# First feed-forward matrix of a two-layer decoder by Strassen's seven block products

## The chip, the cores and the metric

One program on one NeuronCore of a Trainium2 chip. The metric is the device time of one execution in microseconds. In the profile PE is TensorE, DVE VectorE, ACT ScalarE, POOL GpSimd and SP SyncE, which here only issues transfers.

## What is computed

Two layers of a decoder trunk on 1024 prompt tokens and 8 sample tokens, 1032 columns in all. The part that the change touches is the feed-forward block of each layer:

```python
h = _rmsnorm(x, w['norm_ffn_g'][l])
gu = jnp.einsum('bld,df->blf', h, w['ffn_w_up'][l])
gate, up = gu[..., :D_FF], gu[..., D_FF:]
gate, ffn_buf = _causal_dwconv(gate, st_ffn_conv[l], w['ffn_conv_w'][l], w['ffn_conv_b'][l])
x = x + jnp.einsum('blf,fd->bld', jax.nn.gelu(gate) * up, w['ffn_w_down'][l])
```

D_MODEL is 1024 (8 tiles of 128), D_FF 2816 (22 tiles), the convolution has width 3. Ahead of it in a layer stands the mixer: an input projection of 32 tiles, three groups of heads (linear recurrence, retention, state space) and an output projection. It is the same before and after.

## The kernel before

Activations lie feature by token: `x[:, m, :]` is tile m of the residual stream, 128 features by 1032 tokens. Each operand of a large product is split in a high part (rounded to the matmul's fp32r type) and the rest, and each product takes three matmuls (`three`, L695 to L697): high by high, rest by high, high by rest. A token row is cut in NG = 3 groups of 344 columns, since a PSUM bank holds 512.

**Weights.** A slot is 128 x 1024 floats, eight 128 x 128 blocks: one output tile of the first matrix over all of D_MODEL, or a part of the second. SP loads it into one half of `w_raw`, GpSimd splits it into `w_hi` (L674) and `w_lo` (L677) in a loop over all slots of the program, and TensorE frees it. A layer has 44 slots for the mixer and 6 for each of FB = 11 feed-forward blocks.

**Feed-forward blocks.** A block makes two tiles of `gate` and the same two of `up` (four slots, each 8 x 9 matmuls into three PSUM banks), and then two slots of the second matrix for the block ahead of it, eight pieces that are added to `x`. VectorE takes a gate tile out of PSUM with the norm factor `rstd` (L1952), adds two conv taps to what ScalarE's first tap left (L1959, and L1962 for the 8 sample columns), takes the up tiles out (L1970), adds the pieces to `x` (L1992), multiplies gate and up (L1978), and makes the rest of the product's split (L1986). Nine blocks run in a hardware loop; the first and the last are written out.

**The turn.** The mixer's last slots (`out` 5 and two `fin` slots) add the output projection to `x`, tile by tile, in pieces of 344 columns (L1488). As soon as a tile is whole, ScalarE squares it (L1107) and makes the high part of the tile scaled with its norm gain (L1111); VectorE adds the square to `rstd` (L1443) and makes the rest (L1454). `h_hi` and `h_lo` hold all 8 tiles. The division by the token norm comes later, when a product leaves PSUM.

What sets the order is the program of each engine, written by hand, with semaphores between them.

## Time and profile before

| | |
|---|---|
| median of 3 runs | 2878.07 us (2877.52 to 2882.84) |
| span of the profiled execution, first to last instruction | 2875.8 us |
| its own time | not recorded apart; the runs are 1.7 to 7.0 us above the span |
| mean granted TensorE clock | 0.990 |
| TensorE busy | 2817.4 us (98%), 18198 matmuls |
| VectorE, ScalarE, GpSimd busy | 58%, 20%, 36% |
| DMA moved | 228 MB, mean 79 GB/s |

A row that groups instructions names line, engine, operation, output and inputs by the program's names, the shape and the count, then busy time and the mean of one in ns, then the engine's idle time just before them. A source row gives the shortest, middle and longest duration in ns. A timeline row has the start in us, how long it was busy, and what it waited for in brackets. A stretch row has for each engine the busy us and the count, then the granted clock. Matmuls are pipelined: each lasts some 320 ns while one starts every 157, so a pace is read from starts, not from durations.

### The profile page before, as it was taken

To read this page: it belongs to the slowest core of one execution; us is meant where nothing else is said; L and a number is where in the kernel's file an instruction comes from. 1 tells how busy PE (TensorE), PEld (TensorE's weight loads), DVE (VectorE), ACT (ScalarE), POOL (GpSimd) and SP (SyncE) were. 2 spreads that over 40 slices of the span, in tenths; PEclk is the share of its full clock that TensorE was granted. 3 is DMA by queue.
4 is the path that set the end of the run, shared out by engine and by line. 5 is a ranking of instruction groups with operands and counts; after the bars stand their busy time and mean duration, and the time that the engine had idled before them with its cause. 6 is when DMAs were issued, how large, how long until landed. Compare 5 with 4: busy or idle time off the path is not lost.

```text
span 2875.8 us, 46926 instructions
## 1 busy us (share of the span) xinstructions
PE 2817.4 (98%) x18198; PEld 2759.6 (96%) x18198; DVE 1661.4 (58%) x2108; ACT 589.3 (20%) x902; POOL 1022.4 (36%) x440
## 2 busy tenths in 40 slices
PE   9999999899999999999999999998999999999998
PEld 9999999889999999999999999998899999999997
DVE  7659886467344444444746597855664444444447
ACT  4334231123000111001313333211221100111002
POOL 2333323213434434434434333232243443443432
PEclk9999999999999999999999999999999999999998
DMA  4325324411111111111123334344011111111112
GB/s 159 129 79 154 130 92 162 156 33 44 45 51 44 44 51 44 49 46 44 56 89 106 126 113 146 115 135 141 31 46 52 44 46 49 44 47 48 44 52 87
DMA packets 76113, 228.08 MB, mean 79 GB/s; under 512 B 18704, under 2 KB 19728, under 8 KB 74912
## 3 DMA queue, kind: packets, MB, share of 16 engines
q1 hardware_dynamic: 71600, 210.79, 22.5%
q10 hardware_dynamic: 4368, 15.33, 1.7%
q8 instruction: 94, 1.54, 0.2%
q14 instruction: 51, 0.42, 0.0%
HBM read 180.63 MB, written 45.96 MB: 79 GB/s over the span
## 4 chain that ended last, share of the span: by engine, by line
PE 88%; DVE 5%; issue 4%; DMA 1%; ACT 1%; POOL 0%; DVEq 0%; SPq 0%; POOLq 0%; ACTq 0%
PE ps L695 27%; PE ps L697 26%; PE ps L696 26%; DVE sb_pt L1498 2%; PE ps L807 1%; DMA sb_raw<-proj 1%; PE ps L809 1%; PE ps L924 1%; PE ps L863 0%; PE ps L812 0%; PE ps L925 0%; PE ps L830 0%; PE ps L842 0%; PE ps L841 0%; PE ps L882 0%
## 5 line engine op out<-in xcount | busy, mean ns | idle before, releaser
L695 PE MATMUL ps<-sb_h_hi,sb_w_hi 128*128 128x344 f32 x3840 | 1239.6, 323 | 3.5 <-DVE sb_h_lo L1454 1.5
L696 PE MATMUL ps<-sb_h_lo,sb_w_hi 128*128 128x344 f32 x3840 | 1226.3, 319 | 0.0
L697 PE MATMUL ps<-sb_h_hi,sb_w_lo 128*128 128x344 f32 x3840 | 1225.9, 319 | 0.0
L674 POOL TENSOR_TENSOR sb_w_hi<-sb_w_raw,sb_ones 128x1024 fp32r<-128x1024 f32 x218 | 426.2, 1955 | 1795.3 <-PEq L1054 860.4
L695 PEld LDWEIGHTS ps<-sb_h_hi,sb_w_hi 128*128 128x128 f32 x3840 | 722.5, 188 | 12.9 <-issue 7.7
L696 PEld LDWEIGHTS ps<-sb_h_lo,sb_w_hi 128*128 128x128 f32 x3840 | 722.6, 188 | 1.0
L697 PEld LDWEIGHTS ps<-sb_h_hi,sb_w_lo 128*128 128x128 f32 x3840 | 722.5, 188 | 0.0
L677 POOL TENSOR_TENSOR sb_w_lo<-sb_w_raw,sb_w_hi 128x1024 fp32r<-128x1024 f32 x218 | 596.1, 2734 | 17.1
L695 PE MATMUL ps<-sb_y_hi,sb_w_hi 128*128 128x344 f32 x1440 | 476.2, 331 | 20.6 <-DVE sb_x L1488 14.5
L697 PE MATMUL ps<-sb_y_hi,sb_w_lo 128*128 128x344 f32 x1440 | 465.2, 323 | 0.0
L696 PE MATMUL ps<-sb_y_lo,sb_w_hi 128*128 128x344 f32 x1440 | 462.4, 321 | 0.0
L1992 DVE TENSOR_TENSOR sb_x<-ps,sb_x 128x1032 f32<-128x1032 f32 x168 | 207.0, 1232 | 242.3 <-PE ps L697 242.3
L695 PEld LDWEIGHTS ps<-sb_y_hi,sb_w_hi 128*128 128x128 f32 x1440 | 273.5, 190 | 27.0 <-DVE sb_x L1488 16.4
L696 PEld LDWEIGHTS ps<-sb_y_lo,sb_w_hi 128*128 128x128 f32 x1440 | 273.9, 190 | 1.1
L697 PEld LDWEIGHTS ps<-sb_y_hi,sb_w_lo 128*128 128x128 f32 x1440 | 273.7, 190 | 0.0
L1485 DVE TENSOR_TENSOR sb_ev<-ps,sb_rstd 128x344 f32<-128x344 f32 x180 | 89.5, 511 | 218.0 <-PE ps L697 214.3
L1952 DVE TENSOR_TENSOR sb_raw<-ps,sb_rstd 128x1032 f32<-128x1032 f32 x44 | 54.3, 1234 | 255.8 <-PE ps L697 255.5
L1410 ACT ACTIVATE sb_y_hi<-sb_pt 128x1032 fp32r<-128x1032 f32 x40 | 42.9, 1073 | 732.2 <-DVE sb_pt L1978 732.2
L1970 DVE TENSOR_TENSOR sb_pt<-ps,sb_rstd 128x1032 f32<-128x1032 f32 x44 | 54.2, 1233 | 234.6 <-PE ps L697 234.6
L1488 DVE TENSOR_TENSOR sb_x<-ps,sb_x 128x344 f32<-128x344 f32 x264 | 127.0, 511 | 52.5 <-PE ps L697 51.8
L1959 DVE SCALAR_TENSOR_TENSOR sb_pt<-sb_raw,sb_par,sb_pt 128x1024 f32<-128x1024 f32 x88 | 128.0, 1455 | 7.1 <-DVE sb_pt L1962 5.6
L1403 ACT ACTIVATE sb_pt<-sb_raw,sb_par 128x1032 f32<-128x1032 f32 x44 | 55.3, 1256 | 328.8 <-DVE sb_raw L1952 328.8
(256 smaller groups left out, 2249.5 us busy)
## 6 DMA issues: line engine op xcount, KB each, us to landing
sb_w_raw<-w SPq DMA_DIRECT2D x222, 512.0 KB, 3.6
proj<-sb_ev SPq DMA_DIRECT2D x64, 516.0 KB, 3.0
sb_pt<-proj SPq DMA_DIRECT2D x28, 516.0 KB, 5.0
sb_raw<-proj SPq DMA_DIRECT2D x16, 516.0 KB, 4.6
sb_raw<-proj ACTq DMA_DIRECT2D x16, 516.0 KB, 4.2
...
```

The costliest lines, as they stand in the source:

```text
L674: nc.gpsimd.tensor_tensor(w_hi[:, q, :], w_raw[:, q, :], ones[:, 0:1].to_broadcast([P, 1024]), ALU.mult).then_inc(sg.sem("w_hi_done"), 1)
L677: nc.gpsimd.tensor_tensor(w_lo[:, q, :], w_raw[:, q, :], w_hi[:, q, :].bitcast(F32), ALU.subtract).then_inc(sg.sem("w_split_done"), 1)
L695: mm(o, wh, ah, start=first, stop=False)
L696: mm(o, wh, al, start=False, stop=False)
L697: return mm(o, wl, ah, start=False, stop=last)
L1403: af(pt[:, j, :], raw[:, j, 2:T + 2], ACT.Identity, bias=wt[3], scale=wt[2]).then_inc(*sg.on("ffn_tap", (tag, j)))
L1485: v.tensor_tensor(ev[:, EV[i], gc(g)], o, rstd[:, gc(g)], ALU.mult).then_inc(*sg.on(f"p_free{r % NB}", r))
L1488: v.tensor_tensor(x[:, mo, gc(g)], o, x[:, mo, gc(g)], ALU.add).then_inc(*sg.on(f"p_free{r % NB}", r))
L1498: ins = stt(dst[:, 0:SEQ], src[:, k:k + SEQ], w(k), dst[:, 0:SEQ], ALU.mult, ALU.add)
L1952: v.tensor_tensor(g3(raw[:, j, 2:T + 2]), ffn_bank(r)[:, :, 0:TG], g3(rstd[:]), ALU.mult).then_inc(*sg.on("m_free", ("ffn", r)))
L1959: stt(pt[:, j, 0:SEQ], raw[:, j, k:k + SEQ], w, pt[:, j, 0:SEQ], ALU.mult, ALU.add).then_inc(*line.step())
L1992: v.tensor_tensor(g3(x[:, mo, :]), ffn_bank(r)[:, :, 0:TG], g3(x[:, mo, :]), ALU.add).then_inc(*sg.on("m_free", (tag, r)))
```

## The change

It computes the first feed-forward matrix by Strassen's scheme. The product of two output tiles is seen as 2 x 2 blocks: weights A11, A12, A21, A22 (two output tiles by two halves of D_MODEL, 128 x 512 each), activations in two halves of D_MODEL by two halves of the tokens (H = 516). Seven products of four 128 x 128 blocks by 516 columns, each in two groups of HG = 258, take the place of eight. They are called by the activation panel that they use, in the order I1, I5, I2, I6, I7, I3, I4.

- **TensorE.** `product` runs 4 x 2 x 3 matmuls of 258 columns into two banks. `up_pair` runs the seven of a pair, each behind a wait for the eviction that frees its banks; a block has two pairs, gate and up. The second matrix is computed as before, in pieces of 344 columns.
- **Panels.** Instead of `h_hi`/`h_lo`, seven panels `p_hi`/`p_lo` of 4 x 516 columns are made once per layer, at the turn: I1, I2 and I3 are quarters of scaled `x`, I5, I6, I7 and I4 use sums of quarters (t1 to t4). VectorE makes the sums and the rests, ScalarE the high parts. Squares for the norm go through three buffers and are added by GpSimd (tiles 1 to 3) and VectorE (4 to 7). Memory of the mixer is reused for the panels.
- **Weights.** The ring now has three places of 128 x 512, an entry each: 14 entries for a block's first matrix, 4 for its second (22 of either kind in the last block). GpSimd makes four sums for each pair and the rest of every entry; ScalarE makes the high parts (`hi`), each released by the end of the product three entries earlier. SP's loads (three places of 1024) are released by GpSimd's rests.
- **VectorE in a block.** A pair's seven products leave PSUM in seven half-row additions (`c11`, `add_p6`, `c22`, `c12`, `c21`, with a running sum in `tab`). They no longer multiply by `rstd`: the gate tiles are scaled by it in place (`scaled`), and GELU's output too (`scale_gelu`); the product of both is made in `raw` (`times_gelu`).
- **Next layer.** The constants are loaded again in each layer, and GpSimd splits the next layer's first two slots in halves between the last pieces.

```diff
+H = T // 2
+HG = H // 2
+I1, I2, I6, I5, I7, I4, I3 = range(7)
+PER_BLOCK, LAST_ENTRIES = 18, 22
 
...
 
-        pairs = DEPTH * SLOTS // 2 - 1
-        with pool.Fori(0, pairs) as i, sg.loop("split", pairs, i):
-            for q in range(2):
-                pool.wait_ge(sg.sem(f"w_raw{q}"), i * 16 + 32)
-
-                pool.wait_ge(sg.sem(f"w_used{q}"), i + (1 + q))
-                nc.gpsimd.tensor_tensor(w_hi[:, q, :], w_raw[:, q, :], ones[:, 0:1].to_broadcast([P, 1024]),
-                                        ALU.mult).then_inc(sg.sem("w_hi_done"), 1)
-                pool.wait_ge(sg.sem("w_hi_done"), i * 2 + (q + 1))
...
+            def lo(b, e, src):
+
+                r = e if b is None else e + 2
+                pool.wait_ge(*seen("f_hi", layer, b, e + 1))
+                lo_of(w_place(w_lo, r), src, w_place(w_hi, r)).then_inc(sg.sem("f_lo"), 1)
...
+            def up_pair(b, pair):
...
+                nc.gpsimd.tensor_tensor(wsum[:], a21, a22, ALU.add).then_inc(sg.sem("f_sum"), 1)
+                lo(b, e, a11)
+                sums_done(b, n + 1)
+                nc.gpsimd.tensor_tensor(a21, a21, a11, ALU.subtract).then_inc(sg.sem("f_sum"), 1)
+                lo(b, e + 1, wsum[:])
+                sums_done(b, n + 2)
+                los_done(b, e + 2)
+                nc.gpsimd.tensor_tensor(a11, wsum[:], a11, ALU.subtract).then_inc(sg.sem("f_sum"), 1)
+                lo(b, e + 2, a12)
+                sums_done(b, n + 3)
+                los_done(b, e + 3)
+                nc.gpsimd.tensor_tensor(a12, a12, a11, ALU.subtract).then_inc(sg.sem("f_sum"), 1)
+                lo(b, e + 3, a11)
+                lo(b, e + 4, a21)
+                sums_done(b, n + 4)
+                lo(b, e + 5, a12)
+                lo(b, e + 6, a22)
+
...
+            def product(b, bank0, e, panel):
+
+                r = e if b is None else e + 2
+                wh, wl = w_place(w_hi, r), w_place(w_lo, r)
+                entry_ready(b, e)
+                for kk in range(4):
+                    if b is None and e < 7:
+                        pe.wait_ge(*sg.after("pn_lo", (panel, kk)))
+                    w = slice(kk * P, (kk + 1) * P)
+                    for g in range(2):
+                        n = slice(HG * g, HG * g + HG)
+                        ins = three(ps[:, bank0 + g, 0:HG], wh[:, w], wl[:, w], p_hi[:, panel, kk, n],
+                                    p_lo[:, panel, kk, n], kk == 0, kk == 3)
+                        weights_done()
+                ins.then_inc(sg.sem("f_done"), 1)
...
+            def up_pair(b, pair):
+                e, n = 7 * pair, 7 * pair
+                if pair:
+                    pe.wait_ge(*seen("f_ev", layer, b, 5))
+                    if b is None:
+                        pe.wait_ge(*sg.after("rstd_ready", "ffn"))
+                elif b is not None:
...
+                pe.wait_ge(*seen("f_copy", layer, b, pair + 1))
+                product(b, P1_BANK[pair], e + 4, I7)
+                if b is None and pair == 0:
+                    pe.wait_ge(*sg.after("tok_rstd", "ffn"))
+                pe.wait_ge(*seen("f_ev", layer, b, n + 1))
+                product(b, P2_BANK, e + 5, I3)
+                if b is None and pair == 0:
+                    ffn_spread()
+                pe.wait_ge(*seen("f_ev", layer, b, n + 2))
...
+            def hi(b, e, ahead=0):
+
+                if b is not None or e > 2:
+                    act.wait_ge(*seen("f_done", layer, b, turn(e - 3) if e > 2 else e - 2, ahead))
+                elif e != 1:
+                    act.wait_ge(sg.sem(f"w_used{e // 2}"), layer * PAIRS + PAIRS)
...
+            act.wait_ge(*sg.after("sqf_pool", 3))
+            square_f(5, raw[:, 0, 2:T + 2])
+            x_done(7)
+            hi_x(I2, 3, 7, n0)
+            hi(None, 2)
+            rest_panels(3)
+            act.wait_ge(*sg.after("pn_lo", (I4, 1)))
+            square_f(6, fpt[:, 0, :])
+            act.wait_ge(*sg.after("sqf_dve", 5))
+            square_f(7, raw[:, 0, 2:T + 2])
...
+            def up_block(b, blk, tag):
+                if b is not None:
+                    act.wait_ge(*seen("f_done", layer, b, 0))
+                    ys(b, y_hi, -2)
+                copy_p1(b, 0)
+                hi(b, 3)
+                hi(b, 4)
+                hi(b, 5)
...
+                for g in range(NG):
+                    evict(("out", 5, mo, g))
+                diff(mo)
+                if mo >= 1:
...
+                evict(("fin", 5 + kk, 2))
+                rest_lo(kk)
+            square_add(4, tab[:])
+            square_add(5, raw[:, 0, 2:T + 2])
+            lo_x(I2, 3, 7, n0)
+            make_t2(3)
+            make_t3_t4(3)
...
+            def c11(b, pair):
+                piece_done(b, 7 * pair + 3)
+                dve.wait_ge(*seen("f_copy", layer, b, pair + 1))
+                v.tensor_tensor(g2(raw[:, 0, 2:H + 2]), pair_bank(P2_BANK), g2(ta), ALU.add).then_inc(sg.sem("f_ev"), 1)
...
+            def up_block(b, blk, tag):
+                if b is not None:
+                    dve.wait_ge(*seen("f_split", layer, b, 0))
+                c11(b, 0)
...
+                scaled(0, rstd[:]).then_inc(sg.sem("f_gate"), 1)
+                c21(b, 0)
+                scaled(1, rstd[:]).then_inc(sg.sem("f_gate"), 1)
+                conv_gate(blk, tag, 0)
+                conv_gate(blk, tag, 1)
+                c11(b, 1)
+                scale_gelu(tag, 0)
+                add_p6(b, 1)
```

Three places of the engines' orders. First GpSimd in a looped block, where `sb_w_raw`, `sb_w_hi` and `sb_w_lo` are a slot as loaded, its high part and its rest, and `sb_wsum` a sum of two weight blocks. Before:

```order
L674 TENSOR_TENSOR sb_w_hi<-sb_w_raw,sb_ones 128x1024 [waits w_used0]
L676 ISA
L677 TENSOR_TENSOR sb_w_lo<-sb_w_raw,sb_w_hi 128x1024 [waits w_hi_done]
L673 REGISTER_ALU [waits w_raw1]
L674 TENSOR_TENSOR sb_w_hi<-sb_w_raw,sb_ones 128x1024 [waits w_used1]
```

Now, the second pair of a block:

```order
L824 TENSOR_TENSOR sb_wsum<-sb_w_raw 128x512 [waits f_lo,f_raw1,f_raw0]
L807 REGISTER_ALU
L785 TENSOR_TENSOR sb_w_lo<-sb_w_raw,sb_w_hi 128x512 [waits f_hi]
L814 REGISTER_ALU
L827 TENSOR_TENSOR sb_w_raw<-sb_w_raw 128x512 [waits f_sum]
L807 REGISTER_ALU
L785 TENSOR_TENSOR sb_w_lo<-sb_wsum,sb_w_hi 128x512 [waits f_hi]
L814 REGISTER_ALU
L831 TENSOR_TENSOR sb_w_raw<-sb_wsum,sb_w_raw 128x512 [waits f_lo,f_sum]
```

Every instruction has half the width, sums stand between the rests, and each rest waits for ScalarE's high part.

Second VectorE in a looped block, from the last gate eviction to the first of the up tiles. Before:

```order
L1952 TENSOR_TENSOR sb_raw<-ps,sb_rstd 128x1032 [waits ffn_stored1,m_ready]
L1955 ISA
L1959 ISA [waits ffn_tap]
L1959 SCALAR_TENSOR_TENSOR sb_pt<-sb_raw,sb_par,sb_pt 128x1024
...
L1962 SCALAR_TENSOR_TENSOR sb_pt<-sb_par,sb_pt 128x8
L1969 REGISTER_ALU
L1970 TENSOR_TENSOR sb_pt<-ps,sb_rstd 128x1032 [waits m_ready]
```

Now:

```order
L2447 TENSOR_TENSOR sb_raw<-ps,sb_tab 128x516 [waits f_done]
L2411 REGISTER_ALU
L2451 TENSOR_TENSOR sb_raw<-sb_raw,sb_rstd 128x1032 [waits f_ev]
L2454 ISA
L2458 ISA [waits ffn_tap]
L2458 SCALAR_TENSOR_TENSOR sb_fpt<-sb_raw,sb_par,sb_fpt 128x1024
...
L2461 SCALAR_TENSOR_TENSOR sb_fpt<-sb_par,sb_fpt 128x8
L2414 REGISTER_ALU
L2418 REGISTER_ALU [waits f_done]
L2419 TENSOR_TENSOR sb_raw<-ps,sb_tab 128x516 [waits f_copy]
```

A two-operand scaling of `sb_raw` (L2451) is new between them, and what stands behind the eight conv instructions is now `c11` (L2419), which frees banks for the third product after it.

Third ScalarE at the end of the turn (`sb_p_hi` are the panels' high parts, `sb_fpt` and `sb_tab` hold sums, squares and running sums). Now:

```order
L1646 ACTIVATE sb_p_hi<-sb_x,sb_gf 128x516 [waits p_free1]
L1680 ACTIVATE sb_w_hi<-sb_w_raw 128x512 [waits w_used1]
L1651 ACTIVATE sb_p_hi<-sb_raw 128x516 [waits pn_t] x2
L1651 ACTIVATE sb_p_hi<-sb_fpt 128x516 [waits pn_t]
L1732 ISA
L1654 ACTIVATE sb_fpt<-sb_x 128x1032 [waits pn_lo]
L1654 ACTIVATE sb_raw<-sb_x 128x1032 [waits sqf_dve]
L1646 ACTIVATE sb_p_hi<-sb_x,sb_gf 128x516 x4
L1749 ISA
L1754 ACTIVATE sb_tab<-ps 128x516 [waits sqf_dve,f_done]
L1678 REGISTER_ALU [waits f_done]
L1680 ACTIVATE sb_w_hi<-sb_w_raw 128x512 [waits f_sum]
```

The two rows of L1680 are the high parts of entries 2 and 3, for products I2 and I6. The first stands behind the panel of tile 7, the second behind the rest of the panels, two squares and the copy of the first product out of PSUM. Before, the same place:

```order
L1107 ACTIVATE sb_ev<-sb_x 128x1032 [waits sq_used,p_free2]
L1118 REGISTER_ALU
L1111 ISA [waits p_free1]
L1111 ACTIVATE sb_h_hi<-sb_x,sb_gains 128x1032
L1107 ACTIVATE sb_ev<-sb_x 128x1032 [waits sq_used,p_free1]
L1111 ISA
L1111 ACTIVATE sb_h_hi<-sb_x,sb_gains 128x1032
L1125 ACTIVATE sb_rt<-sb_rt 128x9 [waits tok_ms]
```

There ScalarE made only the last tiles' squares and high parts; weights have come in between.

## Rows read from the trace of the kernel before

**Rows 1.** The page: busy time of the engines, and the chain's lines.
```profile
PE 2817.4 (98%) x18198; PEld 2759.6 (96%) x18198; DVE 1661.4 (58%) x2108; ACT 589.3 (20%) x902; POOL 1022.4 (36%) x440
...
PE ps L695 27%; PE ps L697 26%; PE ps L696 26%; DVE sb_pt L1498 2%; PE ps L807 1%; DMA sb_raw<-proj 1%; PE ps L809 1%; PE ps L924 1%; PE ps L863 0%; PE ps L812 0%; PE ps L925 0%; PE ps L830 0%; PE ps L842 0%; PE ps L841 0%; PE ps L882 0%
```

**Rows 2.** Busy time in a stretch of the first layer's feed-forward part.
```profile
core 0: us, PE busy (x) PEld busy (x) DVE busy (x) ACT busy (x) POOL busy (x), PEclk, DMA share, GB/s
760.00:1360.00 600.00, 600.00 (x3826) 600.00 (x3825) 270.91 (x211) 58.86 (x53) 242.41 (x106) 1.00 0.15 47
```

**Rows 3.** Timeline of TensorE, sixteen narrow matmuls and what follows.
```profile
310.98 1.95 PE L863 MATMUL ps<-sb_con,sb_pt 128*128 128x128 f32 x16
312.68 0.40 PE L695 MATMUL ps<-sb_h_hi,sb_w_hi 128*128 128x344 f32 x1
```

**Rows 4.** Source lines of GpSimd's rests and of two VectorE products.
```profile
L677 POOL TENSOR_TENSOR sb_w_lo<-sb_w_raw,sb_w_hi x218: 2347/2406/4263, 31.5 to 2831.8; 128x1024 fp32r<-128x1024 f32 x109
L1978 DVE TENSOR_TENSOR sb_pt<-sb_pt x44: 1850/2134/3444, 730.4 to 2810.6; 128x1032 f32<-128x1032 f32 x44
L1986 DVE TENSOR_TENSOR sb_y_lo<-sb_pt,sb_y_hi x40: 1221/1227/1236, 735.5 to 2768.9; 128x1032 fp32r<-128x1032 f32 x40
```

**Rows 5.** Timeline of GpSimd, one slot.
```profile
797.04 1.89 POOL L674 TENSOR_TENSOR sb_w_hi<-sb_w_raw,sb_ones 128x1024 fp32r<-128x1024 f32 x1 [6.95 <-PEq L1054]
799.01 3.29 POOL L677 TENSOR_TENSOR sb_w_lo<-sb_w_raw,sb_w_hi 128x1024 fp32r<-128x1024 f32 x1
```

**Rows 6.** Timeline of VectorE, the same place.
```profile
798.05 5.34 DVE L1978 TENSOR_TENSOR sb_pt<-sb_pt 128x1032 f32<-128x1032 f32 x2
803.31 1.22 DVE L1986 TENSOR_TENSOR sb_y_lo<-sb_pt,sb_y_hi 128x1032 fp32r<-128x1032 f32 x1
```

**Rows 7.** Source lines of VectorE: additions from PSUM, conv taps.
```profile
L1992 DVE TENSOR_TENSOR sb_x<-ps,sb_x x168: 1219/1233/1234, 777.1 to 2851.7; 128x1032 f32<-128x1032 f32 x168
L1488 DVE TENSOR_TENSOR sb_x<-ps,sb_x x264: 494/511/519, 131.9 to 2101.7; 128x344 f32<-128x344 f32 x132
L1959 DVE SCALAR_TENSOR_TENSOR sb_pt<-sb_raw,sb_par,sb_pt x88: 1279/1286/1964, 707.7 to 2792.6; 128x1024 f32<-128x1024 f32 x88
L1962 DVE SCALAR_TENSOR_TENSOR sb_pt<-sb_par,sb_pt x88: 225/227/2267, 709.7 to 2794.0; 128x8 f32<-128x8 f32 x88
```

**Rows 8.** Source lines of ScalarE: 1032 and 512 columns.
```profile
L1107 ACT ACTIVATE sb_ev<-sb_x x40: 1047/1068/1073, 17.3 to 2853.0; 128x1032 f32<-128x1032 f32 x40
L1202 ACT ACTIVATE sb_ch<-sb_ch x32: 630/631/636, 258.5 to 1835.7; 128x512 f32<-128x512 f32 x32
```

**Rows 9.** The page: DMA issues of the weight slots.
```profile
sb_w_raw<-w SPq DMA_DIRECT2D x222, 512.0 KB, 3.6
```

**Rows 10.** Busy time in the first layer's turn.
```profile
668.00:700.00 32.00, 32.00 (x215) 31.96 (x215) 20.27 (x20) 6.56 (x7) 14.62 (x6) 1.00 0.22 53
```

**Rows 11.** Timeline of VectorE in that turn.
```profile
668.78 2.69 DVE L1443 TENSOR_TENSOR sb_rstd<-sb_rstd,sb_ev 128x1032 f32<-128x1032 f32 x1
671.39 3.43 DVE L1454 SCALAR_TENSOR_TENSOR sb_h_lo<-sb_x,sb_gains,sb_h_hi 128x1032 fp32r<-128x1032 f32 x1
```

**Rows 12.** Timeline of TensorE behind an idle stretch in the mixer.
```profile
573.11 0.65 PE L695 MATMUL ps<-sb_y_hi,sb_w_hi 128*128 128x344 f32 x1 [4.99 <-DVE sb_x L1488]
573.56 0.49 PE L696 MATMUL ps<-sb_y_lo,sb_w_hi 128*128 128x344 f32 x1
573.85 0.49 PE L697 MATMUL ps<-sb_y_hi,sb_w_lo 128*128 128x344 f32 x1
```

**Rows 13.** Busy time and granted clock around it.
```profile
560.00:568.00 8.00, 8.00 (x57) 7.61 (x55) 5.56 (x5) 3.83 (x5) 5.16 (x2) 1.00 0.85 290
573.00:582.00 9.00, 8.08 (x27) 7.64 (x28) 6.72 (x11) 0.26 (x1) 0.00 (x0) 0.50 0.17 58
```

More of the change, by code:

```diff
@@ new lines, in _ @@
+            with sp.Fori(0, LOOPED) as b, sg.loop("ffn", LOOPED, b):
+                ffn_up_weights(b)
+                for j in range(2):
+                    gate_row(b, j, "loop")
+                taken(b, 12)
+                ffn_weights(b, 5)
+            ffn_up_weights(LOOPED)
+            for j in range(2):
+                gate_row(LOOPED, j, "end")
+            taken(LOOPED, 12)
+            ffn_weights(LOOPED, 5)
+            taken(LOOPED, 13)
+            ffn_weights(LOOPED, 6)
+            taken(LOOPED, 15)
@@ new lines, in mixer_left, with ffn_sums @@
+            def mixer_left(bank0):
+                for b_ in range(bank0, bank0 + 2):
+                    last = max(r for r in RING.values() if r % NB == b_)
+                    pe.wait_ge(*sg.after(f"p_free{b_}", last))
+            def ffn_sums():
+                pe.wait_ge(*sg.after("sqf_dve", KD - 1))
+                pe.wait_ge(*seen("f_ev", layer, None, 1))
+                for c in range(NCH + 1):
+                    s = slice(c * CHUNK, min((c + 1) * CHUNK, T))
+                    ins = mm(ps[0:s.stop - s.start, 2, c:c + 1], rstd[:, s], ones[:, 0:1], start=True, stop=True)
+                ins.then_inc(*sg.on("tok_sum", "ffn"))
@@ L1115, in refresh @@
             square(m, key)
[L1116 to L1120 removed]
+            if m == KD - 2:
+                act.wait_ge(sg.sem("f_done"), layer * PIECES + PIECES)
             part(m, g, key)
@@ L1418, in A_dyn, with copy_p1 @@
                 return out
-            ffn_block(0, "first", 0)
-            with act.Fori(0, LOOPED) as b, sg.loop("ffn", LOOPED, b):
-                ffn_block(b + 1, "loop", b * 12 + 4)
-            ffn_block(FB - 1, "end", END + 4)
-            for m in range(KD):
-                act.wait_ge(*freed(layer, END + 12 + m))
-                refresh(m, layer * 2 + 2, "next")
+            def copy_p1(b, pair):
+                act.wait_ge(*seen("f_done", layer, b, 7 * pair + 1))
+                if b is not None or pair:
+                    act.wait_ge(*seen("f_ev", layer, b, 7 * pair - 1))
+                else:
+                    act.wait_ge(*sg.after("sqf_dve", 4))
+                af(g2(ta), pair_bank(P1_BANK[pair]), ACT.Identity).then_inc(sg.sem("f_copy"), 1)
@@ new lines, in _ @@
+            up_block(None, 0, "first")
+            for e in range(3):
+                hi(0, e)
+            with act.Fori(0, LOOPED) as b, sg.loop("ffn", LOOPED, b):
+                up_block(b, b + 1, "loop")
+                for e in range(14, PER_BLOCK):
+                    hi(b, e)
+                for e in range(3):
+                    hi(b, e, 1)
+            up_block(LOOPED, FB - 1, "end")
+            for e in (14, 15, 16):
+                hi(LOOPED, e)
+            ys(LOOPED, p3_hi, 0)
@@ L1427, in _, with next_tile @@
+            hi(LOOPED, 17)
+            hi(LOOPED, 18)
+            def next_tile(m):
+                act.wait_ge(*d_freed(layer, LOOPED, 5 + m))
+                refresh(m, layer * 2 + 2, "next")
+            next_tile(0)
+            hi(LOOPED, 19)
+            next_tile(1)
+            next_tile(2)
+            hi(LOOPED, 20)
+            next_tile(3)
+            hi(LOOPED, 21)
+            for m in range(4, KD):
+                next_tile(m)
         root("last")
@@ L2005, in _, with evicted, piece_done @@
-            up_part(FB - 1, "end", END + 4, 0)
-            for j in range(2):
-                y_product("end", END + 7, 0, (j,))
-                down(j, END + 8 + j, 0, "end")
-            y_rest("end")
-            for mo in range(2, 4):
-                down(mo, END + 8 + mo, 0, "end")
-            dve.wait_ge(*sg.after("ffn_split", "end"))
+            def evicted(b, n):
+                dve.wait_ge(*seen("f_ev", layer, b, n))
+            def piece_done(b, n):
+                dve.wait_ge(*seen("f_done", layer, b, n))
@@ new lines, in _ @@
+            y_rest(LOOPED, -2, y_hi, y_lo, 0).then_inc(sg.sem("f_split"), 1)
+            y_rest(LOOPED, -2, y_hi, y_lo, 1).then_inc(sg.sem("f_split"), 1)
+            up_block(LOOPED, FB - 1, "end")
+            times_gelu(0)
+            times_gelu(1)
+            y_rest(LOOPED, 0, p3_hi, p3_lo, 0).then_inc(sg.sem("f_split"), 1)
+            down(LOOPED, 0, 0)
+            y_rest(LOOPED, 0, p3_hi, p3_lo, 1).then_inc(sg.sem("f_split"), 1)
+            for p in range(1, 4):
+                down(LOOPED, p, p)
@@ L2013, in _ @@
+            dve.wait_ge(*seen("f_split", layer, LOOPED, 2))
             v.nop().then_inc(*sg.on("par_free"))
```

726 lines of the change are left out of this document (511 added, 215 removed).

## The prediction

> **What bounds the kernel now.** I read the page's busy shares and chain first. TensorE is busy 98% of the span, and 79% of the chain that ended last is the three lines of the helper `three` [rows 1]. Then I asked for the feed-forward stretch alone: in 600 us of it TensorE is busy for all 600 and runs 3826 matmuls, one per 156.8 ns, at full granted clock [rows 2]. The reader should see that nothing there waits: VectorE has 271 us of work, ScalarE 59, GpSimd 242. So TensorE's instruction stream is the time, and what it drops is gained, as long as the other three keep up. The change asks much more of all three, so the question is where TensorE starts to wait.
>
> **TensorE's saving.** A pair of output tiles takes 2 x 8 x 3 x 3 = 144 matmuls of 344 columns. At 156.8 ns that is 22.58 us. After the change it takes 7 x 4 x 2 x 3 = 168 matmuls of 258 columns. Their price has no row. 344 columns at 2.4 GHz are 143.3 ns, so 13.5 ns are over. If these belong to the instruction, 258 columns cost 107.5 + 13.5 = 121.0 ns. If they go with the width, 117.6 ns. Sixteen matmuls of only 128 columns take 1.70 us from the start of the first to the start of what follows, 106 ns each [rows 3], so the pace can go well below both. Upper end, an estimate with half again as much over: 128 ns. I take 121.0: 20.33 us per pair, 2.25 us saved. With 22 pairs in each of 2 layers that is **-99 us**. The ends are -124 (117.6) and -47 (128).
>
> Here a rule speaks: the Trainium skill, "TensorE: Matmul & The Clock Gate", Back-to-back issue gap, gives N/2.4 + 2.5 ns. For 344 columns that is 145.8 ns, where the rows show 156.8, so the trace doesn't agree. For 258 columns it would give 110.0 ns, and a saving of 180 us instead of 99.
>
> **The port that VectorE and GpSimd share.** Two VectorE lines do the same thing in size and operands: L1986 always takes 1.22 to 1.24 us, L1978 1.85 to 3.44 [rows 4]. The timeline shows why. GpSimd's L674 ends at 798.93. The first L1978, due at 798.05, ends at about 800.0, and GpSimd's L677, which started at 799.01, takes 3.29 us instead of 2.35 to 2.41. The second L1978 then lasts until 803.39, about 1.1 us after L677 has ended. L1986 follows alone in 1.22 [rows 5, 6]. So a VectorE instruction with two SBUF operands and any GpSimd instruction exclude each other, each for its whole length. One with a PSUM operand is untouched: 168 of L1992 lie between 1.219 and 1.234 us [rows 7]. The skill's "SBUF — State Buffer", section on the two sides of SBUF, calls the shared pair an exclusive lock held for the whole instruction; the trace agrees, and by that rule this change, which loads GpSimd and adds two-operand instructions, collides in every block.
>
> GpSimd's prices: 2.35 us undisturbed for 1024 columns [rows 4]. Half of that is 1.17, the low end for 512. ScalarE takes 1.07 for 1032 columns and 0.63 for 512 [rows 8], a fixed part of some 0.2 us. With that much I get (2.35 - 0.2)/2 + 0.2 = 1.27; with twice as much 1.37, the high end. VectorE: 1.23 for 1032 columns, 0.51 for 344, so 0.70 for 516; conv taps 1.29 and 0.23 [rows 7].
>
> **The loop.** In a block of 14 products (14 x 24 x 0.121 = 40.6 us) GpSimd has 8 sums and 14 rests, 22 x 1.27 = 28 us. VectorE's two-operand instructions there are 6 x 1.23, 4 x 1.29 and 4 x 0.23, 13.5 us. Together 41.5 us of port for 40.6 us of products: just full. The place where it bites is VectorE's order. Product 7 ends at 20.3 us, and VectorE gets it at 20.5. Then come c21 0.70, one scaling 1.23, eight conv instructions 6.1, and only then c11 of the second pair, 0.70, whose eviction frees the bank of product 13: 8.7 us, plus GpSimd's turns. Nine of them need the port. GpSimd issues 11 instructions per 20 us, so about 6 stand in the way: 7.6 us. c11 ends at 36.8, TensorE wants to go on at 12 x 2.90 = 34.8: 2.0 us late. 20 blocks have this place: **+40 us**. Ends: 0 (three turns) and +108 (eight turns of 1.37). ScalarE's 14 high halves (0.63 each) have room in a block, since it was 10% busy [rows 2]; SP's six loads of a block stay six of 512 KB, now each released by a finished rest; one lands in 3.6 us [rows 9], against 9 us between two. I count both at nothing; where a load came late, GpSimd would stand behind it and TensorE behind GpSimd.
>
> **The turn to the feed-forward part.** Before, TensorE runs through it without a gap: 32.0 of 32 us busy [rows 10], though two port collisions stretch L1443 to 2.69 and L1454 to 3.43 us [rows 11]. After, VectorE makes 28 panel rests and 16 panel sums. (a) For each of the last four output tiles it has 3 x 0.52 + 7 x 0.72 = 6.6 us, plus turns behind GpSimd's 2.35 us additions into `rstd`; TensorE brings such a tile in 36 x 0.157 = 5.6. Some 2 us late per tile, **8 us**. (b) Two products (5.8 us) can start early. Product 3 needs a weight piece whose high half stands on ScalarE behind tile 7's panel, which waits for VectorE's last two sets, 13 us, of which TensorE covers 5.8: about **8 us** of idle. (c) Product 4 needs the next piece. Its high half stands behind three panels, two squares, four panels and a PSUM copy: 1.9 + 2.1 + 2.9 + 0.6 = 7.5 us, and behind VectorE's last set and two additions, some 5 us. Then 0.6 and 1.27 us for the piece itself: it is ready 14.4 us after product 3's piece has begun on ScalarE. That piece takes 1.9 itself and product 3 takes 2.9, so TensorE idles about **10 us**. (d) The rest of the first pair loses 2. In all 28 per layer, **+56 us**; ends 30 and 84.
>
> **The clock.** After an idle stretch of 5 us the rows show half clock for the whole of 573 to 582 us, and matmuls 287 ns apart [rows 12, 13]. Gaps (b) and (c) are each longer. If each costs 3.5 us of lost speed, **+14 us**; ends 0 and +30.
>
> **The layer's end.** The last block's pieces come one by one, and GpSimd splits the next layer's two slots in halves between them: 5 us per layer, **+10 us** (0 to 20), an estimate from two late pieces each.
>
> The reload of the constants lies beside the first products of the layer: nothing.
>
> **Sum.** -99 + 40 + 56 + 14 + 10 = +21 us on the span of 2875.8. The median of the runs is 2.3 above that span, so 2878 + 21 = **2899 us**. A measurement of this kernel can tell about 0.2%, 6 us, from no change.
>
> **Rivals.**
> - *The 13.5 ns over are gone with the narrower matmul* (107.5 ns). The saving is 44 x (22.58 - 18.06) = 199 us. But a block's products then take 36.1 us and the port needs 41.5, so each block is 5 us late (100), and the turn hides less (62). -199 + 100 + 62 + 14 + 10 = -13: **2865**. For it: at half clock the pitch is 287 ns = 344/1.2, with nothing over [rows 12]. Against: at full clock it is there in the mean of 3826. 11%. This is the other side: it decides from about 114 ns down, given the waits above. The skill's "TensorE: Matmul & The Clock Gate" would have 2.5 of the 13.5 ns stay: 18 us less saved.
> - *GpSimd at half the width takes half the time* (1.17 us) and meets VectorE four times, not six: c11 ends at 20.5 + 8.7 + 4.7 = 33.9, in time. +21 - 40 = -19, with a little of it left: **2863**. 12%.
> - *ScalarE's and VectorE's turn is covered better*, half of (b) and (c) gone: -28 with the clock: **2871**. 6%.
> - *The port saturates* (1.37 us, or more fixed cost per instruction than I give): 22 x 1.37 + 13.5 = 43.6 us for 40.6, so each block is 4.5 late: +50: **2950**. For it: every instruction now waits for a partner on another engine. 13%.
> - *The change doesn't save what it says*: 128 ns, -47 instead of -99: **2951**. 5%.
> - Forecast, with its own range of 2878 to 2925: 53%.
>
> **Numbers.** The range 2858 to 2948 takes in the three faster rivals and the forecast's own range, and leaves out about half of the last two and a tail below. Faster by over 0.2% (under 2872) are most of the first three rivals: 0.26. Within 0.2%: 0.06, from their upper edges and the forecast's lower one. Slower: 0.68.
>
> **What the profile after would show.** Right: matmuls of 258 columns 121 ns apart; in the loop one gap of about 2 us per block, ended by VectorE's eviction line L2419; GpSimd near 1.27 us for 512 columns, longer where L2451 or L2458 run; at each turn two gaps of 8 to 10 us, ended by GpSimd's L785, with half clock after them. Wrong: a pitch under 117, gaps of L785 in every block (the weights themselves late), or a turn that costs under 15 us.

## The result and the profile after

The changed kernel takes **2852.0 us** (median of 4 runs, 2849.6 to 2852.5) against 2877.9 before: ratio 0.9908, 95% interval 0.9896 to 0.9921. It is 26 us faster, where 21 us slower was forecast, and lies 6 us below the range.

The page, against [rows 1]; then the feed-forward stretch, against [rows 2]:

```profile
PE 2735.3 (96%) x19254; PEld 2668.2 (94%) x19254; DVE 1978.6 (69%) x2478; ACT 867.3 (30%) x1392; POOL 1308.0 (46%) x766
```

```profile
760.00:1360.00 600.00, 593.41 (x4519) 590.96 (x4519) 404.64 (x356) 172.91 (x244) 372.33 (x248) 1.00 0.16 49
```

TensorE now has 6.6 us of idle time in 600, where it had none; VectorE went from 271 to 405 us, ScalarE from 59 to 173, GpSimd from 242 to 372. Its largest waits for other engines, over the whole span (us in total, how often, the longest):

```profile
PE ps L889 <- POOL sb_w_lo L785: 35.1, 14, 7.7
PE ps L889 <- DVE sb_x L1882: 20.5, 12, 5.0
PE ps L889 <- DVE sb_raw L2419: 12.8, 18, 0.9
```

L785 is GpSimd's rest of a weight entry; 29.6 of its 35.1 us are the two gaps at each turn. L2419 is `c11` in the loop, 18 times in 20 blocks. L1882 is the mixer's addition to `x`, some 6 us of it at the two turns.

**The loop.** Successive second-matrix blocks begin 67.79 us apart before and 64.00 after. In this stretch the 258-column matmuls start 119.95 ns apart and the 344-column ones 157.4 (mean of over 1100 each, gaps left out): 336 x 0.11995 + 144 x 0.1574 = 62.97. The 1.03 us left are waits. VectorE's timeline in one block, from the scaling of the second gate tile (L2451) over the eight conv instructions to `c11`, shows where they come from, with GpSimd's beside it:

```profile
903.36 2.24 DVE L2451 TENSOR_TENSOR sb_raw<-sb_raw,sb_rstd 128x1032 f32<-128x1032 f32 x1
905.52 2.31 DVE L2458 SCALAR_TENSOR_TENSOR sb_fpt<-sb_raw,sb_par,sb_fpt 128x1024 f32<-128x1024 f32 x1
908.01 1.00 DVE L2461 SCALAR_TENSOR_TENSOR sb_fpt<-sb_par,sb_fpt 128x8 f32<-128x8 f32 x1 [0.18 <-DVE sb_fpt L2458]
909.17 2.15 DVE L2458 SCALAR_TENSOR_TENSOR sb_fpt<-sb_raw,sb_par,sb_fpt 128x1024 f32<-128x1024 f32 x1 [0.16 <-DVE sb_fpt L2461]
911.48 1.02 DVE L2461 SCALAR_TENSOR_TENSOR sb_fpt<-sb_par,sb_fpt 128x8 f32<-128x8 f32 x1 [0.16 <-DVE sb_fpt L2458]
912.41 1.27 DVE L2458 SCALAR_TENSOR_TENSOR sb_fpt<-sb_raw,sb_par,sb_fpt 128x1024 f32<-128x1024 f32 x1
...
914.22 2.34 DVE L2458 SCALAR_TENSOR_TENSOR sb_fpt<-sb_raw,sb_par,sb_fpt 128x1024 f32<-128x1024 f32 x1 [0.15 <-DVE sb_fpt L2461]
916.71 0.23 DVE L2461 SCALAR_TENSOR_TENSOR sb_fpt<-sb_par,sb_fpt 128x8 f32<-128x8 f32 x1
916.91 0.70 DVE L2419 TENSOR_TENSOR sb_raw<-ps,sb_tab 128x516 f32<-128x516 f32 x1
```

```profile
906.90 2.09 POOL L835 TENSOR_TENSOR sb_w_raw<-sb_w_raw 128x512 f32<-128x512 f32 x1
908.95 3.52 POOL L785 TENSOR_TENSOR sb_w_lo<-sb_w_raw,sb_w_hi 128x512 fp32r<-128x512 f32 x2
```

Six instructions are stretched, that is, they take longer than alone: 1.01 + 1.02 + 0.77 + 0.86 + 0.79 + 1.05 = 5.5 us, against 1.23, 1.29 and 0.23. In each of the eighteen looped blocks there are six, 5.4 to 5.6 us in all. The ends meet: the small tap due at 908.01 ends at 909.01, and GpSimd's L835 at 908.99; the one due at 911.48 ends at 912.50, and GpSimd's pair of rests at 912.47. `c11` ends at 917.61, and TensorE, on its timeline, goes on behind it:

```profile
917.74 0.38 PE L889 MATMUL ps<-sb_p_hi,sb_w_hi 128*128 128x258 f32 x1 [0.77 <-DVE sb_raw L2419]
```

**The turn.** TensorE's timeline in the first layer, and busy time with granted clock behind each of the two gaps:

```profile
698.88 0.58 PE L889 MATMUL ps<-sb_p_hi,sb_w_hi 128*128 128x258 f32 x1 [7.13 <-POOL sb_w_lo L785]
...
711.20 0.58 PE L889 MATMUL ps<-sb_p_hi,sb_w_hi 128*128 128x258 f32 x1 [7.65 <-POOL sb_w_lo L785]
```

```profile
698.88:702.20 3.32, 3.32 (x15) 3.32 (x16) 3.32 (x3) 0.00 (x0) 2.09 (x1) 0.50 0.00 0
711.20:715.90 4.70, 4.70 (x22) 4.70 (x23) 1.19 (x4) 0.00 (x0) 2.80 (x2) 0.50 0.18 31
```

Both gaps and the half clock behind them stand where the prediction put them. A third stretch at half clock, which it did not have, runs from 719.4 to 722.8 us: no gap is ahead of it, but the narrow token sums (L1244, matmuls of one column) end at 718.2. The first addition of the second matrix comes at 798.9 us instead of 777.1 [rows 7]. Of these 21.8 us 0.9 were there ahead of the turn; four pairs have saved 9.6 and one looped block has waited 1.0, so the turn costs 21.8 - 0.9 + 9.6 - 1.0 = 29.5 us per layer. Of it 7.6 are matmuls at half clock (their starts beyond the full-speed pace, 640 to 790 us: 9.3 against 1.7 before), 22 are gaps. Some 3 of these 22 are small waits from 751 to 763 us, at the end of the first block and in the first looped one.

### The profile page after: what moved, and what is told of

The parts are those of the page before. It is cut to its first block, busy times and chain, and to the rows that moved or that the text cites. A ratio compares the mean times of both kernels' runs of the same rounds, so it can differ in the third digit from the quotient of the medians.

```text
span 2850.6 us, 52195 instructions
## 1 busy us (share of the span) xinstructions
PE 2735.3 (96%) x19254; PEld 2668.2 (94%) x19254; DVE 1978.6 (69%) x2478; ACT 867.3 (30%) x1392; POOL 1308.0 (46%) x766
## 4 chain that ended last, share of the span: by engine, by line
PE 53%; issue 17%; DVE 14%; POOL 11%; DMA 2%; ACT 1%; DVEq 0%; POOLq 0%; SPq 0%; ACTq 0%
PE ps L889 16%; PE ps L891 15%; PE ps L890 15%; POOL sb_w_lo L785 7%; DVE sb_fpt L2458 2%; DVE sb_pt L1892 2%; DVE sb_x L1882 1%; DMA sb_w_raw<-w 1%; POOL sb_w_raw L835 1%; POOL sb_wsum L824 1%; POOL sb_w_raw L831 1%; DVE sb_ch L1960 1%; PE ps L1118 1%; POOL sb_w_raw L827 1%; PE ps L1024 1%
## 5 line engine op out<-in xcount | busy, mean ns | idle before, releaser
L785 POOL TENSOR_TENSOR sb_w_lo<-sb_w_raw,sb_w_hi 128x512 fp32r<-128x512 f32 (+1 forms) x352 | 650.0, 1849 | 470.8 <-ACT sb_w_hi L1680 463.2
L889 PE MATMUL ps<-sb_p_hi,sb_w_hi 128*128 128x258 f32 (+1 forms) x2560 | 736.7, 288 | 47.9 <-POOL sb_w_lo L785 35.1
L891 PE MATMUL ps<-sb_p_hi,sb_w_lo 128*128 128x258 f32 (+1 forms) x2560 | 731.1, 286 | 0.0
L890 PE MATMUL ps<-sb_p_lo,sb_w_hi 128*128 128x258 f32 (+1 forms) x2560 | 730.1, 285 | 0.0
L889 PE MATMUL ps<-sb_h_hi,sb_w_hi 128*128 128x344 f32 x1632 | 534.6, 328 | 10.5 <-DVE sb_x L1882 6.2
L889 PEld LDWEIGHTS ps<-sb_p_hi,sb_w_hi 128*128 128x128 f32 x2560 | 488.4, 191 | 55.0 <-issue 47.2
L890 PE MATMUL ps<-sb_h_lo,sb_w_hi 128*128 128x344 f32 x1632 | 523.1, 321 | 0.0
L891 PE MATMUL ps<-sb_h_hi,sb_w_lo 128*128 128x344 f32 x1632 | 521.7, 320 | 0.0
L890 PEld LDWEIGHTS ps<-sb_p_lo,sb_w_hi 128*128 128x128 f32 x2560 | 489.7, 191 | 0.0
L891 PEld LDWEIGHTS ps<-sb_p_hi,sb_w_lo 128*128 128x128 f32 x2560 | 487.8, 191 | 0.0
L1680 ACT ACTIVATE sb_w_hi<-sb_w_raw 128x512 fp32r<-128x512 f32 x260 | 162.3, 626 | 506.4 <-PE ps L891 506.4
```

The costliest lines, as they stand in the source:

```text
L785: return nc.gpsimd.tensor_tensor(o, a, h.bitcast(F32), ALU.subtract)
L889: mm(o, wh, ah, start=first, stop=False)
L890: mm(o, wh, al, start=False, stop=False)
L891: return mm(o, wl, ah, start=False, stop=last)
L1680: af(w_place(w_hi, e if b is None else e + 2), src, ACT.Identity).then_inc(sg.sem("f_hi"), 1)
```

## The experiments

Each is compared with the kernel before in the same session, whose median lay between 2877.7 and 2878.6 us in all of them; differences below are against the changed kernel's 2852.0, which was measured in a session of its own. A single kernel's runs spread over 1 to 9 us, so a difference of 1 to 3 us is not told apart from none.

**1. `c11` ahead of the second tile's taps.**

```diff
                 conv_gate(blk, tag, 0)
-                conv_gate(blk, tag, 1)
                 c11(b, 1)
+                conv_gate(blk, tag, 1)
```

> Edit: on VectorE, in every feed-forward block, the addition that empties the third product's banks of the second pair (c11, L2419) is moved ahead of the second gate tile's conv taps. Theory A (the loop's 0.7 us gaps are c11 standing behind eight conv instructions): the 18 waits for L2419, 12.8 us in all, are gone, nothing else is late, and the time falls by 10 to 13 us, to about 2840. Theory B (VectorE's and GpSimd's chain as a whole is full, and c11 was only the first to show it): the second tile's conv and GELU come 0.7 us later, and with them ScalarE's high part of the last entry that stands behind this GELU; TensorE then waits for GpSimd's L785 instead, some 0.5 us or more per block, and the time stays within 3 us of 2852 or rises.

Measured: 2845.0 us (2843.8 to 2846.4), 7 less. Both theories hold half. The waits for L2419 are gone, and L785 has taken over 16 times:

```profile
PE ps L889 <- POOL sb_w_lo L785: 42.3, 30, 7.6
```

**2. The high part of entry 13 ahead of the second GELU**, on top of 1.

```diff
                 hi(b, 12)
-                gelu(tag, 1)
                 hi(b, 13)
+                gelu(tag, 1)
```

> Edit: c11 ahead of the second tile's conv taps, as in the first run, and on ScalarE the high part of the block's entry 13 ahead of the second GELU instead of behind it. Theory A (in the first run TensorE waited 0.5 us per block for GpSimd's L785 only because ScalarE held entry 13's high part behind that GELU): the loop runs without a wait, another 5 to 8 us off 2845, about 2838. Theory B (VectorE's and GpSimd's chains are full): another wait of the same size comes in its place, within 2 us of 2845.

Measured: 2840.1 us (2834.7 to 2841.3), 12 less than 2852. Blocks are 63.4 us apart instead of 64.0. Theory A holds for the wait it names (L785 is back to 11 waits), but 0.45 us per block of small waits stay, above all 0.2 to 0.3 us for VectorE's L2424 behind `c11`. So two places in the engines' orders were worth 12 of the loop's 21 us.

**3. GpSimd's sums on one column**, in the changed kernel, from the second block on. It leaves out most of the weight sums and so does not compute the products.

```diff
+c_ = slice(0, 512) if b is None else slice(0, 1)
-nc.gpsimd.tensor_tensor(a12, a12, a11, ALU.subtract)
+nc.gpsimd.tensor_tensor(a12[:, c_], a12[:, c_], a11[:, c_], ALU.subtract)
```

and so in the three other sums.

> Of the changed kernel, GpSimd's four weight sums per pair are made on one column instead of 512, in all but the first block (so the seven products are not the reference's): 8 of GpSimd's 22 full-width instructions of a block cost next to nothing. Theory A (VectorE's and GpSimd's instructions exclude each other, and c11 is late by the turns it loses to GpSimd): VectorE's conv taps L2458 fall from a mean of 1.98 us to 1.7 or less, the 18 waits for L2419 (12.8 us) go, and the time falls by 12 to 16 us, to about 2838. Theory B (the stretch comes from something else on VectorE's side, ScalarE's traffic or the waits between its own instructions): L2458 stays near 1.98 us, and so do the waits and the time.

Measured: 2824.2 us (2818.3 to 2826.1), 28 less, twice what was expected: every looped block takes 62.97 us, exactly the two paces' sum, so the loop has no wait left, and 7 us more are won in the first blocks of the two layers, where the small waits from 751 to 763 us are gone. VectorE in the same place:

```profile
896.08 2.31 DVE L2459 SCALAR_TENSOR_TENSOR sb_fpt<-sb_raw,sb_par,sb_fpt 128x1024 f32<-128x1024 f32 x1
898.56 0.23 DVE L2462 SCALAR_TENSOR_TENSOR sb_fpt<-sb_par,sb_fpt 128x8 f32<-128x8 f32 x1 [0.17 <-DVE sb_fpt L2459]
898.95 2.09 DVE L2459 SCALAR_TENSOR_TENSOR sb_fpt<-sb_raw,sb_par,sb_fpt 128x1024 f32<-128x1024 f32 x1 [0.16 <-DVE sb_fpt L2462]
901.20 1.01 DVE L2462 SCALAR_TENSOR_TENSOR sb_fpt<-sb_par,sb_fpt 128x8 f32<-128x8 f32 x1 [0.16 <-DVE sb_fpt L2459]
902.13 1.27 DVE L2459 SCALAR_TENSOR_TENSOR sb_fpt<-sb_raw,sb_par,sb_fpt 128x1024 f32<-128x1024 f32 x1
...
906.63 0.70 DVE L2420 TENSOR_TENSOR sb_raw<-ps,sb_tab 128x516 f32<-128x516 f32 x1
```

From the start of the first tap to `c11` it is 10.55 us instead of 11.39, and the scaling ahead takes 1.23 instead of 2.24. Four instructions are stretched instead of six. The wide taps, though, stay at a mean of 1.97 us (1.98): that figure of theory A was wrong. Fewer instructions on GpSimd shorten the small taps (0.49 us for 0.69; 28 of 88 are stretched for 50). Of the wide ones 62 of 88 are stretched in both kernels: they still meet the rests that are left.

**4. Weight entries 2 and 3 early**, on ScalarE at the turn.

```diff
             hi_x(I2, 2, 6, n0)
+            hi(None, 2)
+            hi(None, 3)
             rest_panels(2)
...
             hi_x(I2, 3, 7, n0)
-            hi(None, 2)
```

> Edit: on ScalarE, at the turn, the high parts of weight entries 2 and 3 are made ahead of the panels of tiles 6 and 7, instead of behind tile 7's panel and behind all panels, two squares and the first product's copy. Theory A (the two gaps of 7.1 and 7.7 us are ScalarE's order): the gap at product 4 goes; the one at product 3 shrinks only by some 2 us, since VectorE makes tile 7's rest only at 699.8 to 701.5 us. About 9 us per layer and half-clock time with it: 18 to 22 us less than 2852, about 2832. Theory B (VectorE is as late as the weights): the wait moves to the token norm, which needs VectorE's last square at 708 us, or to the first product's copy; then some 5 us per layer are left of it and the time is about 2842.

Measured: 2850.7 us (2849.6 to 2851.0), 1 less. Theory B, and further than it said. The gap of product 3 is 6.2 us, now by VectorE's last addition to `x` (L1884), and product 4's gap has gone on to the token sums:

```profile
PE ps L889 <- DVE sb_x L1884: 9.3, 4, 6.2
PE ps L1244 <- DVE sb_raw L2421: 7.3, 1, 7.3
```

(TensorE's waits from 640 to 810 us.) So ScalarE's order, which the prediction priced, was real, but VectorE stood nearly as late right behind it.

**5. The same, and squares 4 and 5 behind tile 7's panel sums.**

```diff
-            square_add(4, tab[:])
-            square_add(5, raw[:, 0, 2:T + 2])
             lo_x(I2, 3, 7, n0)
             make_t2(3)
             make_t3_t4(3)
+            square_add(4, tab[:])
             rest_lo(3)
+            square_add(5, raw[:, 0, 2:T + 2])
```

> Edit: the one of the run before, and on VectorE the two additions of squares 4 and 5 (2 x 1.23 us, the second stretched to 2.11) are moved behind tile 7's panel sums. Theory A (VectorE's rest of tile 7 is what products 3 and 4 now wait for): another 3 us per layer, 6 us less than the run before. Theory B (the norm's sum at the end of the same VectorE chain is what is waited for): the order inside the chain doesn't matter, same as the run before within 2 us.

Measured: 2848.9 us (2846.0 to 2849.9), 2 less than run 4: inside theory B's 2 us; these two squares' place in VectorE's chain hardly matters.

**6. Runs 1 and 5 together.**

> All three edits at once. If the loop and the turn are independent, the gains add: 2852 - 12 - 24 = about 2816 by the theories A. By the theories B of both places: 2842 to 2850.

Measured: 2842.8 us (2840.4 to 2845.8). The gains of the two places add within the spread (7 + 3 for 9), and the time is that of the theories B.

**7. GpSimd's work at the turn on one column**, in the changed kernel: the three additions into `rstd` (L802) and three sums of the first pair. It leaves out most of the norm's sum and of these weight sums.

```diff
-nc.gpsimd.tensor_tensor(rstd[:], rstd[:], a, ALU.add)
+nc.gpsimd.tensor_tensor(rstd[:, 0:1], rstd[:, 0:1], a[:, 0:1], ALU.add)
```

> Of the changed kernel, GpSimd's three additions into rstd and three of its four weight sums of the layer's first pair are made on one column (so the norm and four products of that pair are not the reference's). In the changed kernel VectorE is busy without a pause from 655 to 712 us of the first layer, 58.9 us, of which 15.4 are stretches of its instructions beyond their shortest. Theory A (at the turn VectorE is the bound, and a good part of that is turns lost to GpSimd): VectorE's turn gets some 8 to 10 us shorter, TensorE's gaps at products 3 and 4 fall with it, and the time is about 2852 - 16 = 2836. Theory B (ScalarE's order or VectorE's own work is the bound): less than 3 us per layer, 2846 or more.

Measured: 2834.6 us (2832.9 to 2836.4), 17 less; theory A had 2836. TensorE's timeline at products 3 and 4 has 4.3 and 5.9 us of waits where 7.1 and 7.7 were, and the waits for L1882 fell by 6 us over the span:

```profile
PE ps L890 <- DVE sb_x L1883: 14.5, 6, 5.0
```

VectorE makes `c11` at 702.4 us instead of 712.0, of which 1.8 were there when the turn began. Both gaps still end with L785, whose entry's high part waits on ScalarE for VectorE's sums; thinner work on GpSimd, which was busy for 26 of 57 us, made VectorE's chain shorter, and the gaps with it. So at the turn VectorE is the bound. In the changed kernel it is busy all through the 57 us before `c11` but for 1.8:

```profile
655.00:712.00 57.00, 39.10 (x247) 37.83 (x247) 55.22 (x66) 28.34 (x43) 26.47 (x14) 0.89 0.06 19
```

and some 15 of them are stretches of its instructions beyond their shortest. The thin instructions gave 8 back.

**8. VectorE's turn reordered**, on top of runs 2 and 5: tile 7's three additions to `x` ahead of tile 6's panels, `c11` ahead of the I3 rests (on ScalarE the first copy ahead of the I3 high parts), the token sums behind product 5.

```diff
                 evict(("fin", 5 + kk, 0))
+                if kk == 2:
+                    evict(("fin", 5 + kk, 1))
+                    evict(("fin", 5 + kk, 2))
...
-                if b is None and pair == 0:
-                    ffn_sums()
                 pe.wait_ge(*seen("f_copy", layer, b, pair + 1))
                 product(b, P1_BANK[pair], e + 4, I7)
+                if b is None and pair == 0:
+                    ffn_sums()
```

> Edit: the four edits so far, and four at the turn that only change VectorE's order and what asks for it: tile 7's three pieces are added to x ahead of tile 6's panels; c11 of the first pair comes ahead of the four I3 rests (on ScalarE the first product's copy ahead of the I3 high parts); TensorE's token sums come behind product 5 instead of product 4. Theory A (at the turn TensorE waits for single late VectorE instructions): the gap at product 3 falls from 6.2 us to under 2, the one at the token sums from 7.3 to under 3, some 8 us per layer, and the time is about 2842.8 - 6 (the loop) - 16 = 2821. Theory B (VectorE's whole work of the turn, which ends at 712 us, is the bound, wherever TensorE is made to wait for it): the gaps move to products 4 to 6 and their sum falls by less than 3 us per layer: about 2833.

Measured: 2837.2 us (2834.2 to 2843.3), some 3 less than run 2, inside its spread: as theory B says, the gap moved, here to 3.9 us inside product 3 and to 5.7 us at product 5, though the latter ends with L785 of entry 4, which stands behind four panels on ScalarE.

**9. Entry 4's high part and the first copy early**, on top of run 8.

```diff
             hi(None, 3)
+            hi(None, 4)
             rest_panels(2)
...
             square_f(6, fpt[:, 0, :])
+            act.wait_ge(*seen("f_done", layer, None, 1))
+            act.wait_ge(*sg.after("sqf_dve", 4))
+            af(g2(ta), pair_bank(P1_BANK[0]), ACT.Identity).then_inc(sg.sem("f_copy"), 1)
```

> Edit: the kernel of the run with VectorE's reordered turn, and on ScalarE the high part of entry 4 right behind entry 3's, and the first product's copy behind square 6 instead of square 7. There TensorE waited 5.7 us at product 5 for GpSimd's L785 (entry 4, whose high part stood behind four I3 panels), with VectorE's squares done at 707.7 us. Theory A (these 5.7 us were ScalarE's order alone): product 5 starts at 705.3 us and the token sums at 708.8, product 6 some 6 us earlier: 2837 - 12 = 2825. Theory B (VectorE's whole turn is the bound): product 6 needs the norm and VectorE's I3 rests, and the wait moves there: 2 us per layer at most, about 2833.

Measured: **2829.3 us** (2827.5 to 2829.5, 5 runs), ratio to before 0.9827 (0.9814 to 0.9841): the fastest kernel here that computes all of it, 22.7 us under the changed one. It lies between the theories. Products 4 and 5 now run without a gap; what TensorE waits for from 640 to 730 us is VectorE everywhere:

```profile
PE ps L889 <- DVE sb_p_lo L2344: 4.9, 1, 4.9
PE ps L889 <- DVE sb_x L1888: 4.8, 4, 1.7
PE ps L889 <- DVE sb_y_lo L2108: 2.8, 1, 2.8
PE ps L889 <- DVE sb_rt L1867: 2.3, 1, 2.3
PE ps L1244 <- DVE sb_raw L2424: 1.0, 1, 1.0
```

It is 11 us under run 2. Run 8 holds the edits of runs 4 and 5, which had won 3 us, and is 3 us under run 2, so its own edits won nothing by themselves; run 9's brought 8 more. Whether that edit pays without those of run 8 was not tried.

**10. Twice as many matmuls of half the width.** The four blocks are added up inside each column group, so the order of the additions changes too: twelve matmuls in a row add to the same columns, where it was three and then three to the other group.

```diff
-                    for g in range(2):
-                        n = slice(HG * g, HG * g + HG)
+                for g, lo_, hi_ in ((0, 0, 130), (0, 130, 258), (1, 0, 130), (1, 130, 258)):
+                        n = slice(HG * g + lo_, HG * g + hi_)
```

> Of the changed kernel, each product is made in column groups of 130 and 128 instead of 258, so with twice as many matmuls. It measures what a matmul costs that doesn't go with its width. A straight line through the two measured paces (119.9 ns at 258 columns, 157.1 at 344) has 8.3 ns fixed and 0.433 ns per column: 64.2 ns per matmul here, and the first matrix would take 22 x 2 x (336 x 0.0642 - 20.15) = 62 us more: 2914. With the 12.4 ns over 2.4 GHz at 258 columns all fixed: 66.2 ns, 2943. If a matmul with new weights can't start within some 106 ns of the one before, as sixteen of 128 columns in the kernel before: 35.6 us per pair, and 2852 + 680 = 3530.

Measured: 3713.5 us. All three guesses miss, the third by the least. Busy time in a stretch of 20 us and one of 100, and two pairs of neighbours from the timeline:

```profile
780.00:800.00 20.00, 20.00 (x95) 20.00 (x96) 1.83 (x2) 4.57 (x5) 3.44 (x2) 0.50 0.09 27
1000.00:1100.00 100.00, 100.00 (x839) 100.00 (x838) 43.16 (x41) 20.62 (x28) 39.49 (x28) 1.00 0.10 32
```

```profile
880.06 0.41 PE L890 MATMUL ps<-sb_p_lo,sb_w_hi 128*128 128x128 f32 x1
880.27 0.41 PE L891 MATMUL ps<-sb_p_hi,sb_w_lo 128*128 128x128 f32 x1
...
1000.20 0.27 PE L891 MATMUL ps<-sb_p_hi,sb_w_lo 128*128 128x130 f32 x1
1000.31 0.28 PE L889 MATMUL ps<-sb_p_hi,sb_w_hi 128*128 128x128 f32 x1
```

At full clock the matmuls start 111.6 ns apart (mean of some 670 in each tenth of a millisecond), of 130 columns as of 128; at half clock 213.3. So there is a floor that goes with TensorE's clock, and the straight line through 258 and 344 columns doesn't go on below it. It costs 44 x (336 x 0.1116 - 20.15) = 763 us. The new order of additions is not needed to explain it, for the kernel before shows the same pace with matmuls of one column, the token sums:

```profile
690.73 1.96 PE L775 MATMUL ps<-sb_ones,sb_rstd 128*128 128x1 f32 x18
```

Fourteen of their seventeen starts follow the one before by 111 or 112 ns, at full clock.

The second thing is the clock. Behind the first layer's turn it stayed at half from 698.5 to 978.4 us, though from 720 us on TensorE was busy in all of it, with these narrow matmuls, the token sums and eighteen of 128 columns (L1253), and rose 4 us after the 344-column matmuls of the second matrix had begun. Behind the second layer's turn it stayed at half for only 51 us and rose at 2644.1, right behind L1253's eighteen matmuls, with no 344-column one in sight:

```profile
2620.00:2630.00 10.00, 10.00 (x49) 10.00 (x49) 0.26 (x1) 0.35 (x1) 0.00 (x0) 0.50 0.00 0
2644.00:2650.00 6.00, 6.00 (x54) 6.00 (x55) 2.98 (x4) 1.71 (x2) 0.00 (x0) 0.99 0.02 1
```

In the changed kernel it rose after 3.3 and 4.7 us. What ended the half clock here stays open. Some 1240 narrow matmuls in the first layer and 190 in the second ran at the half-clock pace, 146 us more than at full clock. That is more than the 98 us that are left of the 861 over the changed kernel, since most of the changed kernel's waits in the loop and at the turn are gone (L785 waited for 6.1 us instead of 35.1, L2419 not at all).

## Why the prediction was wrong

The sum had each term in its place, and four of five too dear:

| term | predicted | measured | from |
|---|---|---|---|
| TensorE | -99 | -106 | 44 x (67.79 - 62.97) / 2 |
| loop | +40 | +21 | 20 x 1.03 |
| turn, gaps | +56 | +44 | 2 x 22 |
| half clock | +14 | +15 | 2 x 7.6 |
| layer's end | +10 | +3 | the layer's rest, 1.3 per layer |
| sum | +21 | -23 | measured -26 |

- **TensorE: right, the saving a little low.** 119.95 ns lies between the 121.0 and the 117.6. The rival with 107.5 ns is out, and run 10 shows why it couldn't be: 111.6 ns is the least that even half the width reaches. The trace before could have said so. The 106 ns of [rows 3] are 1.70 us over sixteen, but the last step there is 31 ns, and the other starts are 109 to 112 ns apart. The Trainium skill's "TensorE: Matmul & The Clock Gate", Back-to-back issue gap, gives N/2.4 + 2.5 ns for an isolated matmul, by which an estimate is 110.0 ns at 258 columns and 56.7 at 130, and names some 81 ns per matmul at 128 columns for a stream in which each has its weight load. The runs show 119.95 and 111.6, so neither fits here.
- **The loop: the step that failed.** It said that about six GpSimd instructions stand in the way, "7.6 us". Six did. But each was priced at its whole 1.27 us. VectorE waits for what is left of the instruction that holds the port, 0.92 us in the mean, so 5.5 us for the 7.6. Pauses between its instructions, which the sum did not have, took back some 0.7. `c11` ended 35.3 us into the block instead of 36.8, and TensorE went on at 35.5, where without a wait it would have at 12 x 24 x 0.11995 = 34.5: 0.9 us late instead of 2.0. With 0.1 us of other waits that makes +21 of +40. GpSimd's own price was right: 1.29 us for the 1.27. The place, the releaser and the mechanism were right (runs 1 and 3), and the second limit, product 14's entry behind the GELU, was not seen. With these two waits taken out (run 2) the loop still had 0.45 us per block, and with eight of GpSimd's 22 wide instructions gone (run 3) none: the port is nearly full, as the 41.5 us for 40.6 said.
- **The turn: sizes near, cause half right.** The gaps of products 3 and 4 are 7.1 and 7.7 us for the 8 and 10; the late output tiles (a) cost 3.6 us for the 8, probably since the ring of PSUM banks takes up some of VectorE's lateness (not tried); in run 7, where the additions into `rstd` are thin, the first layer has none of these waits; the rest of the first pair (d) and the pairs behind it cost 3 for the 2. But (c) was priced by what stands ahead of entry 3 on ScalarE; (b) did name VectorE's last two sets. Run 4 took ScalarE's order away and won 1 us: VectorE was nearly as late. Run 7 shows what made it so.
- **Half clock: right** in size, and in place (0.50 behind both gaps) but for the third stretch, which no gap explains.
- **The layer's end** was an estimate without a row, and nearly four times too high.

No single term turns the sign: the loop's 19, the turn's 12, and 7 each of TensorE and the end all went the same way. The 3 us between -23 and -26 are not accounted for. Each unknown was bounded by itself and priced well inside its ends; all the measured terms lie inside their ends, four of the five on the cheap side, and the range was not made for all of them to miss together; the faster rivals, at 0.29 in all, each let a single term go and still ended 11 to 19 us above the result. On the slow side, the rival of a saturated port has a slip: 43.6 us of port for 40.6 of products are 3.0 us late by its own numbers, not 4.5, which is some 2920 instead of 2950.
